# A fill of 28 constant products on TensorE ahead of the first tile of x, in a decoder step on one core

## The reference, cut to what matters

```python
def project(x, g_mix, w_in, b_if):
    h = rmsnorm(x, g_mix)
    z = jnp.einsum('btd,dn->btn', h, w_in)
    qa, ka, va, oa, ia, fa, qb, kb, vb, qc, kc, vc, gates = jnp.split(z, SPLIT_IDX, axis=-1)
...
def rmsnorm(x, g):
    xf = x.astype(jnp.float32)
    y = xf * lax.rsqrt(jnp.mean(xf * xf, axis=-1, keepdims=True) + EPS)
    return (y * g.astype(jnp.float32)).astype(x.dtype)
```

## Time and profile before

| | |
|---|---|
| median of three runs | 963.91 us |
| lowest, highest | 963.64 us, 967.31 us |
| the profiled execution | 964.69 us |
| its span, first to last instruction | 962.9 us |
| TensorE busy | 936.6 us (97%) |
| VectorE, ScalarE, GpSimd busy | 620.1, 413.8, 73.7 us |
| TensorE's granted clock, mean | 1.00 of full |

### The profile page before, as it was taken

One profiled execution on the slowest core, in us unless ns is written; L12 is line 12 of the kernel. 1 busy time (PEld: TensorE's weight loads), 2 busy tenths in 40 slices (PEclk: granted clock), 3 DMA queues, 4 the chain that ended last, 5 costly groups with the idle time before them and its releaser, 6 DMA issues.

```text
span 962.9 us, 18656 instructions
## 1 busy us (share of the span) xinstructions
PE 936.6 (97%) x7381; PEld 913.1 (95%) x7381; DVE 620.1 (64%) x1204; ACT 413.8 (43%) x777; POOL 73.7 (8%) x105
## 2 busy tenths in 40 slices
PE   6999999999999899899999999999999999999997
PEld 6999999999988889899999999999999999999997
DVE  5835556444787464453536678899657998458863
ACT  7433323444544342322222455556324555226553
POOL 0100114011210200020203000000000000000000
PEclk9999999999999999999999999999999999999999
DMA  8583225432221667322222244422421324213212
GB/s 248 136 262 72 51 70 110 161 100 80 74 62 45 153 179 206 92 89 88 88 88 89 88 146 158 173 90 88 132 88 61 116 89 132 88 45 101 87 34 93
DMA packets 104913, 104.78 MB, mean 109 GB/s; under 512 B 11130, under 2 KB 101752, under 8 KB 104492
## 3 DMA queue, kind: packets, MB, share of 16 engines
q1 hardware_dynamic: 101224, 92.51, 32.0%
q0 software_dynamic: 3552, 11.08, 4.0%
q10 hardware_dynamic: 52, 0.01, 0.0%
HBM read 97.74 MB, written 15.45 MB: 118 GB/s over the span
## 4 chain that ended last, share of the span: by engine, by line
PE 84%; DMA 4%; DVE 4%; SPq 4%; ACT 2%; issue 2%; POOL 0%; DVEq 0%; ACTq 0%
PE acc L1373 38%; PE acc L659 34%; SPq L891 3%; DMA G<-gd 2%; PE acc L1278 1%; PE acc L1399 1%; PE acc L1254 1%; PE acc L1132 1%; PE acc L1121 1%; PE acc L1238 1%; ACT h_hi L1873 1%; PE acc L1092 1%; PE acc L1266 1%; PE acc L1487 0%; DVE y_lo L2182 0%
## 5 line engine op out<-in xcount | busy, mean ns | idle before, releaser
L659 PE MATMUL acc<-h_hi,w_hi 128*128 128x288 f32 (+1 forms) x816 | 257.1, 316 | 0.7 <-DVE w_lo L642 0.6
L659 PE MATMUL acc<-h_lo,w_hi 128*128 128x288 f32 (+1 forms) x816 | 235.4, 289 | 0.0
L659 PE MATMUL acc<-h_hi,w_lo 128*128 128x288 f32 (+1 forms) x800 | 229.9, 287 | 0.0
L659 PEld LDWEIGHTS acc<-h_hi,w_hi 128*128 128x128 f32 x816 | 154.5, 189 | 8.4 <-issue 4.6
L659 PEld LDWEIGHTS acc<-h_lo,w_hi 128*128 128x128 f32 x816 | 154.6, 189 | 4.1 <-issue 2.4
L659 PEld LDWEIGHTS acc<-h_hi,w_lo 128*128 128x128 f32 x800 | 150.5, 188 | 0.0
L632 ACT ACTIVATE w_hi<-raw 128x1024 fp32r<-128x1024 f32 (+1 forms) x67 | 70.6, 1053 | 180.2 <-PE acc L659 180.2
L1373 PE MATMUL acc<-h_hi,w_hi 128*128 128x272 f32 x412 | 119.5, 290 | 0.6
L1373 PE MATMUL acc<-h_hi,w_lo 128*128 128x272 f32 x412 | 119.0, 289 | 0.0
L1373 PE MATMUL acc<-h_lo,w_hi 128*128 128x272 f32 x412 | 118.9, 289 | 0.0
L642 DVE TENSOR_TENSOR w_lo<-raw,w_hi 128x1024 fp32r<-128x1024 f32 x66 | 82.8, 1254 | 20.4 <-ACT w_hi L632 18.1
(11 more groups left out here) (402 smaller groups left out, 2035.2 us busy)
## 6 DMA issues: line engine op xcount, KB each, us to landing
raw<-in_w_in SPq DMA_DIRECT2D x25, 1024.0 KB, 5.6
raw<-in_w_gate_up SPq DMA_DIRECT2D x22, 1024.0 KB, 5.1
raw<-in_w_down SPq DMA_DIRECT2D x8, 1024.0 KB, 5.4
rev<-tab POOLq DMA_DIRECT2D x1, 4352.0 KB, 21.8
ring<-in_cache_dsa_kv SPq DMA_DIRECT2D x4, 1024.0 KB, 7.7
raw<-in_w_out SPq DMA_DIRECT2D x4, 1024.0 KB, 5.4
out<-in_cache_dsa_kv SPq DMA_DIRECT2D x2, 2016.0 KB
ring<-in_cache_moba_k SPq DMA_DIRECT2D x48, 64.0 KB, 2.6
```

What stands on the lines that cost most here:

```text
L659: ins = nc.tensor.matmul(acc[:, bank, 0:HALF[half]], a[:, k, :], two(b[:, kx + k, :], half), start=first and k == k0 and c == 0, stop=last ...
```

## The change

Ahead of its wait for the identity, TensorE now waits for the tile of ones and multiplies it with itself 28 times into the first 128 columns of bank 6. Nothing reads the result: the next user of the bank, a transpose of tile 2, starts it anew. No other engine's list is changed.

```diff
@@ -1420,6 +1420,9 @@
                         if i % 2 and k % 2:
                             ins.then_inc(sem("x_tr"), 1)
 
+                pe.wait_ge(sem("pool_set"), SET["ones"])
+                for _ in range(28):
+                    nc.tensor.matmul(acc[:, 6, 0:P], ones[:, :], ones[:, :], start=True, stop=True)
                 pe.wait_ge(sem("con_in"), 16)
                 x_turned(0, range(KD))
                 pe.wait_ge(sem("vec_in"), 64)
```

## The result

The changed kernel takes 966.24 us in the median of 22 runs (965.07 to 968.26), the kernel before 964.40 us (963.11 to 967.31, also 22). The ratio is 1.0017, with a 95% interval of 1.0010 to 1.0024: a loss of 1 to 2.3 us, real but under what the prediction called a change. The profiled execution took 966.83 us, its span is 965.0 us.

What follows compares the result with a forecast made beforehand. TensorE, 97% busy, bounds the kernel, with ScalarE and VectorE setting the pace from 8.21 us. Products end at 9.15, turning adds 1.32, so ScalarE starts at 10.47, not 8.21: 963.9 + 2.3 = 966.2 us, range 964.4 to 968.8.

Steps and rivals of the forecast that it cites:

- what the prediction called a change: Whole kernel: a measurement can tell about 0.5% (4.8 us) from no change; smaller differences count as "same".
- The third rival: TensorE's start: each product is one record, 28 take 5.0 us and fit the wait for tile 0; 963.0 us, chance 0.08.
- The fill: The 28 products on TensorE from 1.0 us: 18 records at the lower level, 38 x 0.112 us, ending at 9.15.
- The first rival: TensorE's start: the clock does not rise under the products, which end at 13.15 us; +7.15 us, 971.1, chance 0.10.
- From the end of the fill to the copy of the vectors: TensorE turns tile 0 and the vectors at the upper level: 1.32 us instead of 2.21, so ScalarE starts at 10.47.
- All that follows moves by the same amount: ScalarE's and VectorE's lists up to block 1 move by 2.26 us; block 1's first product goes from 21.46 to 23.7.
- The faster clock behind the fill: Transposes of tiles 2 and 3 (1.2 instead of 2.05 us) and ten block 0 records speed up; none of it counts.
- The second rival: Before block 0: clock rises, then falls while TensorE turns tiles and waits; 1.2 to 2.2 us more, 967.4 to 968.4, chance 0.12.
- The sentence on the Trainium skill: TensorE's clock: transposes do not count as busy time for it as products do; the trace was said to agree.
- Nothing later takes it back: From block 1 to the end: no later stage absorbs the start's shift, so the end moves by the full 2.26 us.

Runs made afterwards that it cites:

- the run that held the clock: Changed kernel plus 12 more products behind the first six pieces of tile 2, in TensorE's idle time before block 0: 968.14 us against 965.07, ratio 1.0029.
- ten products: Kernel before with the vectors turned ahead of tile 0, and 10 products of the tile of ones ahead of both: 964.31 us against 965.07, ratio 1.0003.
- the order alone: Kernel before with the vectors turned ahead of tile 0 instead of behind it, no products added: 964.71 us against 965.07, ratio 0.9997.

## Why the prediction was right, point by point

The predicted median was 966.2 us in a range of 964.4 to 968.8, and the measured one is 966.24. The hit is closer than the terms deserve, and in part luck: the forecast added 2.3 us to 963.9, the median of three runs, and the measured difference is 1.8 us, on a median of 964.4 over 22. In the two traces block 1 was 3.36 and 1.75 us late, forecast 2.26.

- The number of records (56 for 28 products) and the start (1.01): as worked out. The spacing at the upper level came out at 0.113, forecast 0.112; the lower level was 0.21. The third rival, one record a product, is out.
- The fill: forecast 8.15 us with a rise after 3.9 us. Measured 9.30 and 7.70 in two traces, with rises after 6.3 and 2.9, and 9.28 in the run that held the clock, whose first 28 products are the same. The price of a record was right; the moment of the rise, a single term, is not one number, and its spread of some 3.4 us moves the fill by 1.6 us. The value that I took lies between the two.
- The first rival, no rise at all, did not happen in any trace with 14 products or more. With ten, the clock did not rise under the fill, and with no fill 8.4 us of transposes passed before a rise.
- From the end of the fill to the copy of the vectors: forecast 1.32 us, measured 1.24 (10.31 to 11.55, and 8.70 to 9.94).
- All that follows moves by the same amount: this holds better than anything else in the document. From the copy of the vectors to block 1 it was 13.25 to 13.27 us in each of the eight traces that turn tile 0 first, from the kernel before to the one with 56 products.
- The faster clock behind the fill brings nothing: right for block 0 at block 1's start, as the run that held the clock shows. It is not quite nothing for the turning: of the 2.21 us from tile 0 to the copy, 0.97 came back, which the sum had counted. With 14 products that covered the overrun whole.
- The second rival: the clock did fall again before block 0, as its condition said, but its price was not paid. The rise came after 12 records of block 0 in one trace and after 16 in the other; in the first the second half was held back by `h_lo` anyway, in the second TensorE was ready only some 0.2 us before `w_lo`. My 1.2 us and more were for 32 records at the lower level. Two or three more of them would have begun to cost, so this rival was closer than the result tells.
- The sentence on the Trainium skill (TensorE: Matmul & The Clock Gate, "Part 4: PE-mode transpose") does not hold for the float32 transposes of this case: 56 of them raised the clock 4.4 us after the first, and full transposes were what ran before the rise at 10.3 with ten products. The measurement decides. That the trace agreed with it, as the prediction says, read too much from one start.
- "Nothing later takes it back": in the profiled pair block 1 was 3.36 us late and the end 2.1. The missing 1.2 us need not be slack that the change used up. From block 1 to the end, the ten traces take 940.2 to 943.4 us, with no clear order in the size of the shift: 942.0 with the latest block 1 (29.64), 943.4 and 941.5 with two of the earliest (20.81 and 20.79), 941.4 in the kernel before, 940.2 in the changed one. (The five latest starts average 941.3 and the five earliest 942.1, less apart than single traces are.) The two traces of the kernel before and of the wait alone, the same work, drifted apart by 0.7 us more between 320 and 373 us, where TensorE waits for transfers of cached values, and back by 0.4 later. One trace of each kernel can tell the start to 0.1 us and the end only to about 1.5. By the runs, the loss with 56 products (4.1 to 7.4 us) is less than the 8.2 and 8.8 us by which block 1 was late in its trace. This claim of the prediction is therefore not settled: the traces fit it, the runs do not show it.

What stays open: why the 22 runs put the loss at 1.0 to 2.3 us, near the small end of the 1.75 to 3.97 of the traces. The starts of the other runs are not seen. Early rises in them would explain it, but of the three traces of this fill two have the late one; slack in a later stage would too. And 14 products lost 1.3 us (0 to 2.5) without a late start. A series of traces of one kernel would tell, and was not made.

## What to carry to other kernels

A fill on an in-order engine must end before what it waits for arrives, reckoned at the lower clock and not at the upper. Otherwise the overrun, less what a faster clock gives back behind it (0.97 us here), makes the stage behind it late: here 28 products of 0.23 to 0.43 us each stood in a hole of 5 us. And a faster clock is only worth something on an engine that ends the waits of its stage: look for the row behind which the stage really starts (here `w_lo`, and behind it the copy of the vectors), and, before pulling that forward, for the transfer that stands just behind it.

## What the runs showed of the hardware that was not expected

- The moment at which the clock rises under unbroken work differs between executions of one program: 2.9 and 6.3 us after the first product for the changed kernel. With 56 and 14 products it was 3.1 and 4.5, and with the order alone 8.4 us of transposes, eight of them small, stood before it.
- Full 128 x 128 transposes of float32 raise it too (4.4 us after the first of 56).
- The granted clock is printed as 1.00 from the start of the trace, also where the spacing of 0.21 us shows the lower level; 0.50 is printed only after the clock has been up and fallen, as at 18 to 19 us of the changed kernel, where the spacing is the same 0.21. For the first rise one has to read the distances of the starts.
- The moment of the fall differs as well. In the first trace of the changed kernel the first transposes after the hole of 2.73 us still came at the upper level, and the granted clock, 0.73 in the mean from 17 to 18 us and 0.50 after, fell at about 17.5 (0.54 us of that stretch at 0.50), some 0.8 us after TensorE had resumed at 16.68. In the second trace, with a hole of the same length (12.34 to 15.07), it fell inside it, at about 14.1 (0.54 in the mean from 14 to 15 us). With 14 products, where holes of 0.66, 0.58 and 1.37 us followed each other, it fell at about 12.1, inside the last.
